# A fourth weight buffer and two experts per loop body in the expert stage of a hybrid decoder kernel

## The reference

```python
def _moe(xn, router, w_gu, w_down):
    logits = (xn @ router).astype(jnp.float32)
    top_v, top_i = lax.top_k(logits, TOP_K)
    w = jax.nn.softmax(top_v, axis=-1)
    gates = jnp.sum(w[..., None] * jax.nn.one_hot(top_i, N_EXPERTS, dtype=jnp.float32), axis=-2)
    y = jnp.zeros_like(xn)
    for e in range(N_EXPERTS):
        y = y + gates[..., e:e + 1].astype(xn.dtype) * _swiglu(xn, w_gu[e], w_down[e])
    return y
```

## Time and profile before

| what | value |
|---|---|
| runs, median (lowest to highest) | 1589.74 us (1588.81 to 1589.75) |
| profiled execution, its own time | 1592.62 us |
| its span in the trace | 1590.9 us |
| mean granted TensorE clock | 0.964 |
| expert stage, start of the first and end of the last matmul | 506.00 us, 1567.26 us |
| busy: TensorE, VectorE, ScalarE | 1467.7, 1128.7, 957.1 us |
| TensorE's matmuls, and as many weight loads | 7417 |

### The profile page before, as it was taken

The page is one execution under the profiler, slowest core; times in us unless marked ns, Lnnn a source line. Parts: engine busy times, 40 slices in busy tenths (PEclk is TensorE's granted clock), DMA queues, the critical chain, the costliest instruction groups (busy, mean ns, idle before and its releaser), DMA issues.

```text
span 1590.9 us, 19935 instructions
## 1 busy us (share of the span) xinstructions
PE 1467.7 (92%) x7417; PEld 1226.2 (77%) x7417; DVE 1128.7 (71%) x840; ACT 957.1 (60%) x745; POOL 53.6 (3%) x78
## 2 busy tenths in 40 slices
PE   6989999999998998999899899899989989989992
PEld 5979999899776787777688678778768867877872
DVE  6764444664555887788588688678858868877884
ACT  4844334443443775777577577577757757757772
POOL 1220000200003000000000000000000000000001
PEclk8999999999999999999899899999989989999996
DMA  9459555693142998899799799889979979997992
GB/s 309 143 204 339 185 185 185 231 313 132 54 146 110 378 367 335 324 372 369 258 375 365 279 362 364 331 309 376 362 261 386 357 275 362 366 347 294 372 337 92
DMA packets 165204, 457.84 MB, mean 288 GB/s; under 512 B 9672, under 2 KB 52784, under 8 KB 165168
## 3 DMA queue, kind: packets, MB, share of 16 engines
q1 hardware_dynamic: 153888, 424.75, 73.1%
q0 software_dynamic: 6336, 23.07, 3.9%
q10 hardware_dynamic: 4944, 9.54, 1.9%
HBM read 432.16 MB, written 25.17 MB: 287 GB/s over the span
## 4 chain that ended last, share of the span: by engine, by line
PE 70%; DVE 10%; ACT 9%; issue 8%; ACTq 1%; DMA 1%; POOL 0%; DVEq 0%; POOLq 0%; SPq 0%
PE bank L1018 22%; PE bank L1020 21%; PE bank L1019 21%; DVE w_lo L629 6%; ACT w_hi L381 6%; DVE hid_lo L989 2%; PE bank L1275 1%; PE bank L1176 1%; ACT silu L579 1%; PE bank L1174 1%; ACT y_sb L609 1%; PE bank L1199 0%; PE bank L1283 0%; ACT L579 0%; PE bank L1189 0%
## 5 line engine op out<-in xcount | busy, mean ns | idle before, releaser
L629 DVE TENSOR_TENSOR w_lo<-raw,w_hi 128x2048 fp32r<-128x2048 f32 x403 | 917.7, 2292 | 363.4 <-ACT w_hi L381 361.5
L381 ACT ACTIVATE w_hi<-raw 128x2048 fp32r<-128x2048 f32 x403 | 767.6, 1915 | 331.4 <-PE bank L1020 320.9
L1018 PE MATMUL bank<-w_hi,act_lo 128*128 128x512 f32 x896 | 361.4, 403 | 25.8 <-DVE w_lo L629 25.8
L1019 PE MATMUL bank<-w_lo,act_hi 128*128 128x512 f32 x896 | 352.2, 393 | 0.0
L1020 PE MATMUL bank<-w_hi,act_hi 128*128 128x512 f32 x896 | 352.2, 393 | 0.0
L1018 PE MATMUL bank<-w_hi,hid_lo 128*128 128x512 f32 x536 | 220.4, 411 | 41.9 <-DVE hid_lo L989 41.9
L1018 PEld LDWEIGHTS bank<-w_hi,act_lo 128*128 128x128 f32 x896 | 170.5, 190 | 77.8 <-DVE w_lo L629 44.2
L1019 PE MATMUL bank<-w_lo,hid_hi 128*128 128x512 f32 x536 | 216.4, 404 | 0.0
L1020 PE MATMUL bank<-w_hi,hid_hi 128*128 128x512 f32 x536 | 216.1, 403 | 0.0
L1020 PEld LDWEIGHTS bank<-w_hi,act_hi 128*128 128x128 f32 x896 | 170.0, 190 | 37.0
L1019 PEld LDWEIGHTS bank<-w_lo,act_hi 128*128 128x128 f32 x896 | 170.9, 191 | 33.5
(11 more groups left out here) (236 smaller groups left out, 974.2 us busy)
## 6 DMA issues: line engine op xcount, KB each, us to landing
raw<-in_moe_w_gu SPq DMA_DIRECT2D x226, 1024.0 KB, 6.5
raw<-in_moe_w_down SPq DMA_DIRECT2D x112, 1024.0 KB, 7.4
raw<-in_mlp_w_gu SPq DMA_DIRECT2D x22, 1024.0 KB, 5.1
raw<-in_mlp_w_down SPq DMA_DIRECT2D x11, 1024.0 KB, 4.9
tok_rows<-zeros POOLq DMA_DIRECT2D x17, 512.0 KB, 11.1
y_rows<-zeros POOLq DMA_DIRECT2D x17, 512.0 KB, 10.6
raw<-in_lru_w_in SPq DMA_DIRECT2D x8, 1024.0 KB, 12.5
raw<-in_w_kvf SPq DMA_DIRECT2D x8, 1024.0 KB, 5.4
```

The source lines that it names most:

```text
L381: a.activation(w_hi[:, u % SPL, :], raw[:, u % RAW, :], ACT.Copy).then_inc(hi_done, 1)
L629: v.tensor_tensor(w_lo[:, u % SPL, :], raw[:, u % RAW, :], w_hi[:, u % SPL, :].bitcast(f32), ALU.subtract).then_inc(lo_done, 1)
L1018: t_.matmul(dst, l_lo, r_hi, start=start, stop=False)
L1019: t_.matmul(dst, l_hi, r_lo, start=False, stop=False)
```

## The change: what it does

- The splits of the expert stage go round four pairs of buffers: the fourth is `alt_hi`/`alt_lo`, which hold the tokens until `gather` is done. Splits run three units ahead (`MLEAD`; `moe_slot`, `moe_hi`, `moe_lo`).
- Each engine's loop body holds two jobs (`expert_pair`); the last pair stands behind the loop, written out.
- `T_AFTER[3]` goes from 39 to 37, `TOK_AFTER` from 37 to 38; token transposes use banks 0 and 1 instead of 6 and 7; the last group's hidden parts lie in spare chunks of `act_hi` and `act_lo`.
- The last job's result isn't stored. Its high and low parts are multiplied by a transposed selection matrix `sel_T` and added to `x` in halves. The other experts' rows are gathered and added during the last job (`ADD_AT`).
- `xs_g` is computed by VectorE behind `tokens_lo(0)` instead of by GpSimd. Unit 2 is split before the tokens. SiLU's table is asked for at the head of each body.
- `ROWS` is 16 x 128 instead of 17 x 128; SyncE loads no units beyond the last job.

```diff
-T_AFTER = (11, 23, 33, 39)
-TOK_AFTER = 37
-ROWS = 17 * P
+T_AFTER = (11, 23, 33, 37)
+TOK_AFTER = 38
+ROWS = 2 * NE * P
+MSPL = 4
+MLEAD = MSPL - 1
+ADD_AT = (14, 17, 21, 25)
...
+        def moe_slot(g):
+            s = (U_MOE % SPL, (U_MOE + 1) % SPL, (U_MOE + 2) % SPL, SPL)[g % MSPL]
+            if s < SPL:
+                return w_hi[:, s, :], w_lo[:, s, :]
+            return alt_hi[:].rearrange("p c n -> p (c n)"), alt_lo[:].rearrange("p c n -> p (c n)")
...
-            pool.wait_ge(gmoe_loaded, 16)
-            for t in range(NT):
-                g.tensor_tensor(xs_g[:, t, :], xs[:, t, :], gmoe_bc[:], ALU.mult).then_inc(xsg_ready, 1)
...
+            def moe_hi(i, g):
+                u, n = U_MOE + g, 2 * J6 * i
+                act.wait_ge(raw_full[u % RAW], raw_count(u, n))
+                act.wait_ge(unit_used, units(u, n) - MSPL + 1)
...
+                    act.wait_ge(unit_used, U_MOE + JU * j + JU)
+                    if final_job:
+                        for half in range(2):
+                            a.activation(y_hi[:, HALF * half:HALF * half + HALF], bank[4 + half], ACT.Copy).then_inc(yhi_done, 1)
...
+                        if final_job and k in ADD_AT:
...
+                            dve.wait_ge(y_back[t][c], 16)
+                            v.scalar_tensor_tensor(out=x[:, t, :], in0=(xs, xs_g)[c][:, t, :], scalar=gate_t[:, c, t:t + 1], in1=x[:, t, :],
+                                                   op0=ALU.mult, op1=ALU.add).then_inc(moe_added, 1)
...
+            v.tensor_copy(sel_T[:], bank[3][:, 0:T]).then_inc(selT_ready, 1)
+            dve.wait_ge(gmoe_loaded, 16)
             for t in range(NT):
+                v.tensor_tensor(xs_g[:, t, :], xs[:, t, :], gmoe_bc[:], ALU.mult).then_inc(xsg_ready, 1)
...
-                if p == NPAIR - 1:
-                    pe.wait_ge(tok_lo_done, KD + j + 1)
-                elif p:
+                if p:
                     pe.wait_ge(e_hid_lo, NPAIR * j + p)
...
+            pair = pe.value_load(last_pair[0:1, 0:1], min_val=NE // 2 - 1, max_val=NE - 1)
+            with pe.Fori(0, pair) as i:
+                expert_pair(i, False)
+            expert_pair(pair, True)
```

More of the change, by code:

```diff
@@ L589, in _ @@
             act.wait_ge(njobs_ready, 1)
[L590 to L612, removed]
+            pair = act.value_load(last_pair[0:1, 0:1], min_val=NE // 2 - 1, max_val=NE - 1)
+            with act.Fori(0, pair) as i:
+                expert_pair(i, False)
+            expert_pair(pair, True)
+            act.wait_ge(x_final, 1)
             squares(4)
@@ L995, in _, with moe_lo @@
-            for t in range(NT):
-                for c, back in enumerate((xs, xs_g)):
-                    dve.wait_ge(y_back[t][c], 16)
-                    last = v.scalar_tensor_tensor(out=x[:, t, :], in0=back[:, t, :], scalar=gate_t[:, c, t:t + 1], in1=x[:, t, :],
+            def moe_lo(i, g):
+                u, n = U_MOE + g, 2 * J6 * i
+                dve.wait_ge(hi_done, units(u, n) + 1)
+                hi, lo = moe_slot(g)
+                v.tensor_tensor(lo, raw[:, u % RAW, :], hi.bitcast(f32), ALU.subtract).then_inc(lo_done, 1)
@@ new lines, in _ @@
+            expert_pair(pair, True)
+            for half in range(2):
+                w = slice(HALF * half, HALF * half + HALF)
+                dve.wait_ge(yhi_done, half + 1)
+                v.tensor_tensor(y_lo[:, w], bank[4 + half], y_hi[:, w].bitcast(f32), ALU.subtract).then_inc(ylo_done, 1)
+            for half in range(2):
+                for t in range(NT):
+                    w = slice(HALF * half, HALF * half + HALF)
+                    dve.wait_ge(scattered, 2 * half + t + 1)
+                    last = v.scalar_tensor_tensor(out=x[:, t, w], in0=bank[2 * t + half], scalar=gate_l[:, t:t + 1], in1=x[:, t, w],
@@ L1245, in expert_in @@
                 unit_ready(u, n)
+                hi, lo = moe_slot(u - U_MOE)
                 kt = 2 if GU_UNITS[p] == 4 else 4
@@ L1263, in expert_out @@
                         first, final = p == 0 and i == 0 and k == 0, p == NPAIR - 1 and i == 1 and k == 1
-                        last = mm3(bank[4 + half], hid_hi[h], hid_lo[h], w_hi[:, u % SPL, w], w_lo[:, u % SPL, w], first, final)
+                        last = mm3(bank[4 + half], h_hi[:, h], h_lo[:, h], hi[:, w], lo[:, w], first, final)
                 last.then_inc(unit_used, 1)
@@ new lines, in _ @@
+            pe.wait_ge(sell_built, 1)
+            for t in range(NT):
+                last = t_.transpose(bank[3][:, t * P:(t + 1) * P], sel_f[:, t, :], ident[:])
+            last.then_inc(sell_T, 1)
+            keep_warm(5, 2)
+            pe.wait_ge(njobs_ready, 1)
+            pair = pe.value_load(last_pair[0:1, 0:1], min_val=NE // 2 - 1, max_val=NE - 1)
+            with pe.Fori(0, pair) as i:
+                expert_pair(i, False)
+            expert_pair(pair, True)
+            keep_warm(6, 6)
@@ L1322 @@
+            for half in range(2):
+                w = slice(HALF * half, HALF * half + HALF)
+                pe.wait_ge(ylo_done, half + 1)
+                for t in range(NT):
+                    dst = bank[2 * t + half]
+                    t_.matmul(dst, sel_T[:, t * P:(t + 1) * P], y_lo[:, w], start=True, stop=False)
+                    t_.matmul(dst, sel_T[:, t * P:(t + 1) * P], y_hi[:, w], start=False, stop=True).then_inc(scattered, 1)
 _INS = ["x", "norm_g", "lru_w_in", "lru_conv_w", "lru_conv_b", "lru_gate_w", "lru_gate_b", "lru_lambda", "lru_w_out",
```

248 lines of the change are left out of this document (159 added, 89 removed).

## The result

The changed kernel takes **1495.94 us** (median of 4 runs, 1491.78 to 1498.65), the kernel before 1589.74 (4 runs beside it). The ratio is 0.9406, with a 95% interval of 0.938 to 0.9431: 94 us less. The forecast was 1495. That the two numbers agree so closely is partly luck: the sum was 6.5 us too high for the execution that it was made against, and one of its main steps named the wrong engine as the one that sets the pace.

What follows compares the result with a forecast made beforehand. With TensorE's pauses gone, DMA was to bound: 633.7 + 6 x 121.0 + 125.2 - 5.0 + 7 x 0.5 = 1483.4, plus tail 13.2, plus 1.7, less 2.9: 1495 us. Range of 8 in 10: 1466 to 1520.

Steps and rivals of the forecast that it cites:

- 8.0 and 7.2: Expert jobs: four split buffers remove 2.36, 2.65 and 3.0 us per job; moved transposes remove 4.57 and 2.65.
- The pace: Expert jobs: DMA at 121.0 us outlasts TensorE at 117.8; 121.0 per job plus 0.5 for late units.
- the term of 3.0 us for late splits: Expert jobs: TensorE's waits below 0.7 us for splits queued behind other work, 3.0 us per job, removed by four buffers.
- rival A: Expert jobs: DMA keeps up and TensorE sets the pace at 117.8 us per job, 1470 as a median; chance 0.24.
- rival C: Expert jobs: a full DMA queue is slower still, 126 us per job, 1527 in all; chance 0.05.
- The last job and the margin: Last job 125.2 us, sharing DMA with gathers; 5.0 us taken off once for units lying ready when DMA becomes later.
- The start: First loop entry: late scatter idles TensorE 10.4 us before unit 3, then 2.6 of slow restart; job 0 ends at 633.7.
- the routing's 3.1 us: Before the jobs: VectorE's small routing instructions without GpSimd's multiplication beside them bring the first matmul from 506.0 to 502.9.
- the microsecond or two in brackets: Before the jobs: a possible further gain of a microsecond or two if shorter routing also spares TensorE its pause there.
- The tail: Kernel's end: from last matmul to end of span 13.2 us instead of 23.6, a gain of 10.4.
- From span to median: Whole kernel: span 1496.6 plus 1.7 gives 1498.3 for such an execution; less 2.9 against the median gives 1495.
- Rival D: Loop bodies of two jobs: instructions fetched again, 36 fetches in all, make the kernel slower than before; chance 0.02.

Runs made afterwards that it cites:

- tok_wait: Against the changed kernel, ScalarE's wait for the token scatter moved from the loop's entry to the token load at unit 10; 1481.47 us, ratio 0.9291.
- best: Changed kernel with padding 16, the third transposes one unit earlier and the scatter wait moved to the token load; 1470.94 us, ratio 0.9223.
- best_half: Changed kernel with padding 16, earlier third transposes and the scatter wait moved, loading only half of each expert unit; 1471.96 us, ratio 0.923.

## Why the prediction was right, and where it was not

**Direction, size and the cause of the gain: right.** The pauses at unit 40 and unit 2 are gone, the granted clock is at 1.00, and undoing either part brings waits back at the places that were named, unit 40 and unit 2. How the gain splits between the parts was not right: each alone gives back some 3.6 us per job, not 8.0 and 7.2.

**The pace: the step that failed.** "With TensorE at 117.8 and DMA at 121.0, DMA is the later one." TensorE was mis-sized, and DMA was no bound. TensorE needs 120.4 us: 30 units of 2.72 (81.6; the gate and up units, and units 40 and 41), 12 down units out of `hid_hi` of 2.81 (33.7), 3.5 of transposes, 0.67 at unit 36, and 0.9 of wider gaps right behind the transposes and that wait. The step took one unit's 2.72 for all 42; the kernel before would not have corrected it, since its down units run at 2.72 too. The change itself made twelve of them slower, by 0.09 x 12 = 1.1 us. The rest is the term of 3.0 us for late splits, of which the prediction kept nothing: 1.6 us of it are still there. (That term was also misread. The stretch of 133 us has 8.5 us of idle time, 6.9 of them in the two long pauses, so only 1.6 were waits; the other 1.4 were wider gaps.) The mechanism was rival A's. Its 1470 missed by the same mis-sized term: 2.5 us on each of seven jobs are 17.5, and with them it would have come to 1488; most of what then lacks is the step from the span to the median, below.

That DMA's 121.0 was no bound has its reason in how it was worked out: busy share times length. Half the bytes gave the same time, and in the changed kernel itself the same full share carried from 375 to 409 GB/s (stretches of 60 us, one in the middle and one in the last job):

```profile
1130.00:1190.00 60.00, 60.00 (x273) 49.57 (x272) 51.81 (x26) 44.13 (x26) 0.00 (x0) 1.00 1.01 392
...
1370.00:1430.00 60.00, 60.00 (x273) 49.57 (x272) 55.17 (x28) 44.14 (x27) 6.97 (x3) 1.00 1.02 409
```

A share near 1 says that transfers are in flight, not that no more would fit. The 358 GB/s of the Trainium skill ("DMA: Bandwidth & Descriptors", Specifications) were exceeded over whole jobs, at 375; the measurement decides, and rival C falls with it.

**The last job and the margin: wrong, and harmless.** 125.2 was forecast for the last job, less 5.0 of margin. The gathers of `y_rows` ran beside it at 409 GB/s, and it took 119.6 (from the copy of job 6, about 1356.5, to 1476.1). Neither term exists when DMA doesn't bind. From job 0's end to the last matmul the forecast had 849.7, and 842.0 were measured.

**The start: right in its sum, off in two terms.** The pause was forecast at 10.4 and is 10.18; job 0 was to end at 633.7, and ScalarE copies its result at 634.08. The first matmul came 2.1 us earlier than the 502.9 forecast: the routing's 3.1 us did come, and so did the microsecond or two in brackets, since TensorE no longer waits 3.27 us for `route` and its ten fillers behind that take 2.40 us instead of 4.59. How much earlier is partly chance, with 500.05 to 503.68 in the other executions. Job 0 needed about 2.5 us more than the 117.8, as every job did, and that used them up.

**The tail.** 13.9 against 13.2: the first halves' split and the matmuls behind them took a little longer.

**From span to median: an error that covered the other.** The sum for the profiled execution was 1498.3, and 1491.8 came. The median of all four runs is 4.2 above that one, where 2.9 below was taken over from the kernel before. The runs of the changed kernel spread over 7 us. The profiles show two parts of such a spread: the first matmul of the stage, which moves by 3.6 us from execution to execution, and the stops at the end of a pair, of 0.2 to 2.6 us, once with a slow stretch behind it.

**Rival D, its premise: half right.** The instruction queue of the earlier trace rows now fetches more than twice as much (the page's list of queues, and the view of DMA from 755 to 995 us, the second pair):

```profile
q8 instruction: 56, 0.92, 0.2%
...
q8 instruction: 10, 0.16, 0.3%
```

Ahead of the expert stage it is 19 packets in both kernels. In the stage the kernel before fetched 4, all in its first job; the changed one fetches 8, 10, 10 and 8 in its four pairs, 36 as the rival had it. So the pair's body is fetched again on each pass. But in the sequence of matmuls the fetches cost nothing: the only stops that end in "issue" stand where a pair's taken branch is, two of them, and not in each execution. The Trainium skill ("Runtime: NRT & Kernel Launch", Instruction fetch mechanics) says that a block's boundary is mostly hidden and that a taken branch whose target is out of the window stalls. The trace agrees on the place; the stop was 0.2 to 2.6 us where there was one, and seven of the thirteen executions have none.

**The xs_g move.** Forecast as a gain of 3.1 ahead of the jobs, which it is (4.8 with the fillers), and as a pause of 13 us with its slow matmuls behind. Taken back alone it changes nothing (1494.59 against 1494.43). The pause doesn't come from the multiplication, but from the wait for the scatter standing ahead of a loop in which nothing needs it for ten units. The forecast priced the pause rightly, and didn't say that it was to be had for one moved line.

## What to carry to other kernels

A busy DMA share multiplied by the length of a stretch isn't a need; before you name DMA as the next bound, look for the highest rate that a full share has delivered, and, once runs are to be had, halve the bytes. Price an engine's need by each kind of unit, and measure it again after the change, since here the units whose tiles only moved took 2.81 us instead of 2.72. And when a wait is placed ahead of a loop or a queue, ask for each instruction behind it whether it needs what is waited for: here one moved wait was worth 13 us, more than each of the other repairs.

## What the runs showed of the hardware that was not expected

- Matmuls with a 128x512 moving operand and `hid_hi` or `hid_lo` as the stationary one follow at 2.72 us per unit of 12 with `hid_hi` at 178560, at 2.81 with it at 178656, and at 2.79 at 178688; in the same executions those out of `act_hi` and `act_lo` stay at 2.72. No wait stands between them, and neither half of the DMA traffic nor three buffers instead of four change it. The cause is open.
- An indirect DMA's issue on GpSimd took 3.09 us instead of 0.98 beside a split on VectorE; in the three executions without the pause at the start (`tok_wait`, `best`, `best_half`), where splits also run beside the scatter, its last two issues took 2.2 and 1.9. In the ten others each issue took 0.96 to 1.09. Small VectorE instructions took 1.14 and 2.32 instead of 0.17 beside a GpSimd multiplication. So each of the two engines was slow beside the other.
- The same pause of 2.67 us ahead of unit 40, with the transposes behind unit 39, was followed by matmuls 0.43 us apart in three of seven jobs: at once in one, and only after about five and six matmuls at full rate in the other two. In four jobs it was followed by none, and so were all waits of 0.67.
- At the taken branch of TensorE's loop the stop was anything between nothing and 2.62 us, at the same place of the same body.
